# Modulation rows beside the branch mixture, six block-product pairs in the first feed-forward stage, ten in the second

## What is computed

```python
def hybrid_layer(x, c_act, ...):
    mod = c_act @ w_ada + b_ada                       # "modulation", 1 x 6144 per layer
    shift1, scale1, gate1, shift2, scale2, gate2 = jnp.split(mod, 6, axis=-1)
    h = modulate(rms_norm(x, norm1_g), shift1, scale1)
    ...
    y_br = jnp.einsum('bsnw,nwd->bsnd', branches, w_br)
    gates = jax.nn.sigmoid(h @ w_mg + b_mg).reshape(b, s, N_BRANCH, D_MODEL)
    mixed = jnp.sum(gates * y_br, axis=2) @ w_o       # the branch mixture
    x = x + gate1[:, None, :] * mixed
    h2 = modulate(rms_norm(x, norm2_g), shift2, scale2)
    u, g = jnp.split(h2 @ w_up, 2, axis=-1)           # 2 x 2816 columns
    u = causal_dwconv(u, w_conv, b_conv)              # three taps over the rows
    y = (jax.nn.silu(u) * g) @ w_down
    return x + gate2[:, None, :] * y
```

## Time and profile before

| what | us |
|---|---|
| median of 3 runs | 2886.88 |
| lowest and highest | 2886.42 and 7420.36 |
| the profiled execution, its time | 2883.55 |
| the profiled execution, its span | 2881.8 |

### The profile page before, as it was taken

How to read it: one execution, slowest core, us unless ns; L and a number is a source line. 1 busy time by engine, 2 the same in 40 slices (tenths; PEclk the granted TensorE clock), 3 DMA queues, 4 the chain that set the end, 5 groups by cost and what they waited for, 6 DMA issues and landing times.

```text
span 2881.8 us, 37607 instructions
## 1 busy us (share of the span) xinstructions
PE 2838.7 (99%) x15707; PEld 2402.4 (83%) x15707; DVE 1618.1 (56%) x2271; ACT 1183.9 (41%) x1809; POOL 1110.5 (39%) x458
## 2 busy tenths in 40 slices
PE   8999999999999999999999999999999999999999
PEld 5777888888888887788898989888999877789998
DVE  6444572467665624422266766647668466676683
ACT  4335333342333424532244435344334466443433
POOL 2332345334444332344434234443334423333432
PEclk9999999999999999999999999999999999999999
DMA  8331353346564422233233333333333322233332
GB/s 258 104 105 50 107 193 110 95 150 201 190 197 124 118 74 59 74 95 96 87 103 88 95 99 100 102 95 92 99 104 102 107 70 66 73 94 97 106 104 76
DMA packets 507293, 314.27 MB, mean 109 GB/s; under 512 B 14290, under 2 KB 478836, under 8 KB 506868
## 3 DMA queue, kind: packets, MB, share of 16 engines
q1 hardware_dynamic: 507124, 311.87, 36.7%
HBM read 309.73 MB, written 2.10 MB: 108 GB/s over the span
## 4 chain that ended last, share of the span: by engine, by line
PE 90%; DVE 6%; ACT 2%; DMA 1%; issue 1%; SPq 1%; POOL 0%; DVEq 0%; ACTq 0%
PE b L495 15%; PE b L497 15%; PE b L496 15%; PE o L495 4%; PE o L497 4%; PE o L496 4%; PE s L495 2%; PE s L496 2%; PE s L497 2%; PE b L1224 2%; PE b L1226 2%; PE b L1225 2%; PE s L1226 1%; PE s L1225 1%; PE s L1224 1%; PE b L1163 1%
## 5 line engine op out<-in xcount | busy, mean ns | idle before, releaser
L3370 POOL TENSOR_TENSOR lo<-raw,hi 128x1024 fp32r<-128x1024 f32 (+2 forms) x448 | 1108.2, 2483 | 1742.0 <-ACT hi L1501 1378.1
L1501 ACT ACTIVATE hi<-raw 128x1024 fp32r<-128x1024 f32 (+2 forms) x451 | 461.4, 1035 | 319.6 <-DMA raw<-in_w_up_dram 90.9
L495 PE MATMUL b<-HH,hi 128*128 128x512 f32 x1312 | 523.9, 399 | 0.0
L497 PE MATMUL b<-HH,lo 128*128 128x512 f32 x1312 | 511.4, 390 | 0.0
L496 PE MATMUL b<-HL,hi 128*128 128x512 f32 x1312 | 511.4, 390 | 0.0
L495 PEld LDWEIGHTS b<-HH,hi 128*128 128x128 f32 x1312 | 246.4, 188 | 58.4 <-issue 7.1
L497 PEld LDWEIGHTS b<-HH,lo 128*128 128x128 f32 x1312 | 246.3, 188 | 52.6
L496 PEld LDWEIGHTS b<-HL,hi 128*128 128x128 f32 x1312 | 246.6, 188 | 50.7 <-issue 1.4
L2521 DVE SCALAR_TENSOR_TENSOR AA<-raw,CA,AA 128x512 f32<-128x512 f32 x140 | 143.1, 1022 | 3.3
L495 PE MATMUL b<-FH,hi 128*128 128x512 f32 (+1 forms) x383 | 140.8, 368 | 0.0
L496 PE MATMUL b<-FL,hi 128*128 128x512 f32 (+1 forms) x383 | 140.6, 367 | 0.0
(11 more groups left out here) (645 smaller groups left out, 6891.8 us busy)
## 6 DMA issues: line engine op xcount, KB each, us to landing
raw<-in_w_up_dram SPq DMA_DIRECT2D x88, 512.0 KB, 4.0
raw<-in_w_ada_dram SPq DMA_DIRECT2D x80, 512.0 KB, 4.9
raw<-in_w_in_dram SPq DMA_DIRECT2D x76, 512.0 KB, 4.0
raw<-in_w_mg_dram SPq DMA_DIRECT2D x48, 512.0 KB, 3.7
raw<-in_ffn_w_gate_dram SPq DMA_DIRECT2D x44, 512.0 KB, 3.8
raw<-in_ffn_w_up_dram SPq DMA_DIRECT2D x44, 512.0 KB, 3.9
raw<-in_w_down_dram SPq DMA_DIRECT2D x32, 448.0 KB, 3.9
raw<-in_ffn_w_down_dram SPq DMA_DIRECT2D x32, 448.0 KB, 4.1
```

The lines of the kernel that those rows point to most:

```text
L495: e.matmul(out, wh, xh, start=start and k == 0, stop=False)
L497: mm = e.matmul(out, wl, xh, start=False, stop=stop and k == last)
L1501: e.activation(t["hi"][:, c % NSLOT, 0:w], K.raw[:, c % NSLOT, 0:w], ACT.Copy).then_inc(*m.hi.up(c))
L3370: e.tensor_tensor(t["lo"][:, s, 0:w], K.raw[:, s, 0:w], t["hi"][:, s, 0:w].bitcast(F32), ALU.subtract).then_inc(*m.lo.up(n))
```

## The change

Three things change. The modulation rows of the second layer are no longer left to the first feed-forward stage: one generator goes on from the first layer's rows to the second's, and the branch mixture of the first layer takes 60 of its steps in place of 28. The first feed-forward stage then makes f = 14, 15, 16, 17, 19 and 20 as pairs (none before) and takes no modulation step at its last block (marked `BUSY`); its input sums stand inside the down group behind f = 7. The second stage has ten pairs in place of thirteen, spaced otherwise. And in all four stages ScalarE's silu of the block before a pair stands behind the copy of "mid" and no longer ahead of it.

```diff
-PAIRS_OF = ((), (6, 7, 8, 9, 10, 12, 13, 14, 15, 16, 17, 19, 20),
+PAIRS_OF = ((14, 15, 16, 17, 19, 20),
+            (7, 8, 9, 11, 12, 14, 15, 16, 18, 19),
             (5, 6, 7, 8, 9, 10, 12, 13, 14, 15, 16, 17, 19, 20),
             (5, 6, 7, 8, 9, 10, 12, 13, 14, 15, 16, 17, 19, 20))
...
-        ada = (y for q in range(4, 12) for y in P.ada(0, q)) if l == 0 else iter(())
+        ada = (y for k, q0 in enumerate((4, 0)) for q in range(q0, 12) for y in P.ada(k, q)) if l == 0 else iter(())
...
-        drain(beside(chain(P.mixing(l, 0, (1,)), *[P.mixing(l, dp, (0, 2, 1)) for dp in (1, 2, 3)]), ada, 28))
+        drain(beside(chain(P.mixing(l, 0, (1,)), *[P.mixing(l, dp, (0, 2, 1)) for dp in (1, 2, 3)]), ada, 60))
...
-        fill = fill_next()
-        weave(P.ffn(l), fill, False)
+        weave(P.ffn(l), ada, False)
...
-                    yield from self.project(ap, c0, key, freed)
+                    for _ in self.project(ap, c0, key, freed):
+                        yield BUSY if f == KF - 1 else None
...
-    def pair_copies(self, i, f):
+    def pair_copies(self, i, f, late):
...
                      scale=-1.0).then_inc(*m.atake.up(("mid", i, f)))
+        if late is not None:
+            self.ffn_silu(i, late)
         q.wait_ge(m.dense.at("mid5", i, f))
...
                     yield from self.tile()
+                    if (i, f, d) == (0, 7, 3):
+                        self.halves_high(i)
...
                     self.down_update(i, DOWN[f][0], d, gate)
+                    if i == 0 and f == 7:
+                        if d == 0:
+                            self.halves_whole(i)
+                        if d == 2:
+                            self.halves_sums(i)
+                        if d in (4, 6):
+                            self.halves_low(i, (d - 4, d - 3))
```

More of the change, by code:

```diff
@@ L420, in schedule @@
         P.order = BIG4
-        drain(beside(chain(P.mixing(l, 0, (1,)), *[P.mixing(l, dp, (0, 2, 1)) for dp in (1, 2, 3)]), ada, 28))
+        drain(beside(chain(P.mixing(l, 0, (1,)), *[P.mixing(l, dp, (0, 2, 1)) for dp in (1, 2, 3)]), ada, 60))
         P.mods(l, 1)
         drain(P.out_proj("w_o", l, P.x_norm(2 * l + 1)))
-        def fill_next(l=l, ada=ada):
-            yield from ada
-            if l + 1 < DEPTH:
-                for q in range(12):
-                    yield from P.ada(l + 1, q)
-        fill = fill_next()
-        weave(P.ffn(l), fill, False)
+        weave(P.ffn(l), ada, False)
         if l + 1 < DEPTH:
             P.mods(l + 1, 0)
-        weave(P.out_proj("w_down", l, P.x_norm(2 * l + 2)), fill)
+        weave(P.out_proj("w_down", l, P.x_norm(2 * l + 2)), ada)
         P.order = BIG3
@@ L2046, in late_tile @@
                 self.pair_high(i, g, part)
-        if f is not None:
-            self.ffn_silu(i, f)
     def ffn(self, i):
@@ L2053, in take @@
             self.ffn_jobs(i, j)
-            if j == 3 and PAIRS_OF[i]:
+            if j == 3 and i:
                 self.halves_high(i)
@@ L2065, in ffn @@
                 for j in (2 * f, 2 * f + 1):
-                    yield from self.tile()
+                    for _ in self.tile():
+                        yield BUSY if f == KF - 1 else None
                     self.ffn_jobs(i, j)
@@ L2072, in ffn @@
                 yield BUSY
-                self.pair_copies(i, f)
+                self.pair_copies(i, f, late)
                 if late is not None:
@@ L3016, in take @@
             self.ffn_jobs(i, j)
-            if PAIRS_OF[i]:
+            if i:
                 if j == 2:
```

## The result

| what | before | after |
|---|---|---|
| median | 2886.42 us (the runs beside the changed kernel) | 2899.21 us (5 runs, 2897.27 to 2899.68) |
| ratio after to before | | 1.0048, 95% interval 1.0037 to 1.0059 |
| the profiled execution | 2883.55 us, span 2881.8 | 2899.21 us, span 2897.4 |

What follows compares the result with a forecast made beforehand. TensorE, busy 2838.7 of 2881.8 us, was taken as the bound. Terms: second stage -6.0, first-stage gains -8.2, its new waits +15.6, `w_o` +1.1, sum +2.5 us; on the median 2886.88 this gave 2889, range 2876 to 2902.

Steps and rivals of the forecast that it cites:

- Second stage, -6.0: Second feed-forward stage: +2.4 us for three pairs fewer, -10.6 for losses gone, +2.2 for two run starts; sum -6.0.
- the 3.7 us and the clock stretch go: Second stage's head and first pairs: with f = 7 first, VectorE finishes its sums early, removing the 3.7 us and slow-clock losses.
- The rival that named this stage: Second stage keeps its waits at run starts 11 and 18 and the head's lag: -6.0 becomes -1, 2894 us; chance 0.06.
- First stage, the input sums, 3.5: Down group behind f = 7: VectorE ends 12.7 us late, slack 8.1, TensorE waits 3.5 us, ends 0 and 12.7.
- Pair 14, 2.9: First stage, start of pair 14: chunks issued late for want of slots, TensorE waits 2.9 us, ends 0 and 5.
- Pair 15, 7.0: First stage, pair 15: late chunks at its start and a late copy of "mid", 7.0 us, ends 1.2 and 10.
- The clock, 1.0: First stage: lower granted clock behind waits of over 2 us adds 1.0 us in all, not 1.6 apiece.
- Pairs at 0.8: Both stages: each pair saves 0.8 us; six more in the first give -4.8, three fewer in the second +2.4.
- the tail at -3.4: First stage's end: modulation rows end earlier, the bank is free but for 0.2 us, the clock stretch goes: -3.4 us.
- Mixture 0, `w_o` +1.1: First layer's mixture: the added steps are hidden, no wait; at `w_o` a late low part costs 1.1 us, ends 0 and 2.
- Most waits don't appear: First stage: VectorE catches up and chunks come earlier, only about four run-start waits remain: about -8.5 us, 2878; chance 0.28.
- VectorE and GpSimd block each other: Down group behind f = 7: GpSimd casts hold up the sums, 31.6 us in place of 21.4: +13.8, 2901; chance 0.12.

Runs made afterwards that it cites:

- rows_only: The changed kernel without the first stage's six pairs and input sums; modulation rows, the second stage's ten pairs and silu's place stay: 2876.35 us, 0.9974 times before.
- banks_of_before: The changed kernel with only the PSUM bank counter moved, 6 behind the first stage and 3 behind the second: 2890.26 us, 1.0020 times before.
- quiet_13: banks_of_before with no modulation step beside f = 13, its two chunks coming four steps later: 2896.35 us, 1.0039 times before.
- silu_only: The kernel before with only silu of the block before a pair moved behind the copy of "mid": 2883.07 us, 0.9996 times before.
- rows_split: Against the changed kernel: second layer's rows 4 to 11 made in that layer, twelve pairs in both stages, least recently used bank: 2881.55 us, 0.9991 times before.
- sums_spread: banks_of_before with the twelve input-sum instructions one at a time, four low parts behind tiles of f = 8 and 9: 2884.09 us, 1.0000 times before.
- split_last: rows_split with more pairs, first-stage pairs from f = 8, input sums one at a time behind the modulation rows, last folds later: 2872.90 us, 0.9959 times before.
- changed_again: The changed kernel run once more, unaltered, to see whether the lower clock comes at the same places: 2899.89 us, a single execution.

## Why the forecast was near, and where it was wrong

In all, 2.5 us were summed and over 13 came. The forecast is near as a time because the change is small against the whole, not because the sum of the change was right. The measured 2899.21 lies inside the range only because the range's upper end was set by the rival in which GpSimd blocks VectorE, and that rival is not what happened: here the range was lucky.

- **Second stage, -6.0.** Right as a sum (rows_only: -6.1, banks_of_before: -5.1) and wrong in this kernel: +3.2. The step that failed is "the 3.7 us and the clock stretch go": they go, but I asked only when VectorE is done for the first pair, and not which bank each tile takes once the first stage has pairs. What came in its place is the wait of 6.3 us for a bank at f = 4 and 2.7 us of lower clock behind it. The rival that named this stage (its waits stay, 2894) had the right stage and the wrong mechanism.
- **First stage, the input sums, 3.5 by the lag read from the ring.** The right path: 4.0 us of waits in the trace, through the late weight DMA. With the clock they cost 5.8 (6.4 without the pairs). The sums took 18.8 us of VectorE, not 21.4.
- **Pair 14, 2.9.** A wait of 2.2 us from the late slot, shown by quiet_13 and by VectorE's idle time ahead of the sums, and 1.6 of lower clock in the profiled execution. The chunks were issued at 761.65 and VectorE's first sum began at 767.31, 5.7 behind; 5.5 had been forecast.
- **Pair 15, 7.0.** 6.8 by the matmul starts: 3.3 at its start (2.6 forecast), 0.8 at the copy where 4.4 had been forecast, and 2.7 of lower clock. The chain itself came as forecast. Tile 6 began at 814.96; the sums of pair 16 and the copy of "mid" were forecast 19 and 23.7 us behind (833.96 and 838.7), timelines of VectorE and ScalarE:

```profile
834.14 1.21 DVE L2953 TENSOR_TENSOR ER<-raw 128x1024 f32<-128x1024 f32 x1
```

```profile
837.82 0.58 ACT L2030 ACTIVATE MP<-s 128x512 f32<-128x512 f32 x1
```

The copy ended at 838.40. TensorE had used up most of that time at the pair's start and at the lower clock, so little was left to wait. No experiment takes this pair apart; it is read from the trace.

- **The clock, 1.0.** Mis-sized: some 6 us in the first stage, and 2.7 in the second where none was forecast. Of the 6, 2.7 lie ahead of pair 15's copy and stand in the place of a wait, as the prediction had it ("a slower TensorE also lets VectorE catch up"). The waits alone (gaps between matmul starts) were 11.0 us where 14.6 had been forecast, so the first stage's sum came out nearly right by two errors of opposite sign.
- **Pairs at 0.8 and the tail at -3.4.** Measured 4.9 for six and 3.97. Of the tail, 1.5 is again clock: in silu_only a wait of 2.15 us at that place was followed by clock 1.00, and `w_down` took 18.8 in place of 20.3. Two things could have taken the wait away, the end of the modulation rows, as forecast, and the bank counter, which gives the tile another bank in after. quiet_13 tells them apart: there the tile and the one that holds its bank are as before (`o` for both), the rows have ended, and the wait is 0.19 us, the 0.2 of the forecast.
- **Mixture 0, `w_o` +1.1.** Right: no wait in the mixture, 0.95 at `w_o` (0.9 to 1.5 in the other kernels).
- **The rivals.** *Most waits don't appear*: refuted. *VectorE and GpSimd block each other*: the mechanism is real (last section), its size was not: the sums took 18.8 us, not 31.6. Its number, 2901, was near by accident.

Of what is left, the +0.67 in the second layer and the +0.8 at the end have a share of the bank counter too: after has a wait of 0.78 us at 1274.94 and one of 1.61 at 2300.70 that neither before nor banks_of_before has. The +0.95 ahead of `w_o` I can't put down to the change: that part took 525.4 to 527.2 in the fourteen traces.

## What to carry to other kernels

A resource handed out by a running counter makes far-away code part of every edit: count what the edit takes from it. Giving out the least recently used one took the wait out of the stages here and put another into the attention mixer, so the banks are to be compared for the whole program either way. On a queue shared by two streams, what mattered here is the longest lump between two uses of a slot, not the mean load: the same twelve instructions cost 5.8 to 6.4 us as lumps of four and nothing when spread. Optional work that shares the ring belongs where nobody's chunks are late for it, and moving it must be followed to the place where it lands.

## What was not expected of the hardware

The lower granted clock (1.2 of 2.4 GHz) is not fixed by the program. Two executions of the same kernel had it behind different waits of about 2 us. One place shows it best: ahead of the attention's output projection all fourteen traces have the same wait for VectorE, 1.88 to 1.90 us; in nine the lower clock followed and the first three tiles took 18.04 to 18.09 us, in five (before, after, rows_split, sums_spread, split_last) it did not and they took 16.45 to 16.47. From the first stage on, every wait of 2.8 us or more in the fourteen traces had it beside or behind it. In three traces (rows_only, silu_only, changed_again) it also came in the attention mixer with no wait of over 0.4 us just ahead; in rows_only nine matmuls of 512 columns lost 1.7 us there:

```profile
2399.60:2403.00 3.40, 3.40 (x9) 2.62 (x9) 1.87 (x3) 2.93 (x8) 0.34 (x1) 0.50 0.04 11
```

From the first stage on it cost 1.5 to 3.0 us each time. Three such stretches more or fewer, an estimate from these prices, make a single profile differ by some 5 us, and of two profiles that differ by less, the gaps ahead of it are to be compared and not the spans. The Trainium skill ("TensorE: Matmul & The Clock Gate", Part 1) says that the number of slow matmuls at a kernel's start differs from run to run; the traces here show the same in the middle of one.

VectorE and GpSimd do block each other, once per cast. Timelines of POOL and VectorE in the trace of after:

```profile
685.93 2.40 POOL L3378 TENSOR_TENSOR lo<-raw,hi 128x896 fp32r<-128x896 f32 x1 [6.53 <-ACT hi L1496]
```

```profile
686.30 2.58 DVE L2521 SCALAR_TENSOR_TENSOR AA<-raw,CA,AA 128x512 f32<-128x512 f32 x1
```

The multiply-add takes 0.75 us alone. Here it began 0.4 us after a cast had begun and ended at 688.88, 0.55 behind the cast's end at 688.33: but for 0.2 us of its work it stood still until the cast was through. The Trainium skill ("SBUF — State Buffer", two separate sides) states an exclusive lock for the whole instruction, between a GpSimd instruction that reads SBUF and a VectorE one with two SBUF inputs, and the trace agrees but for these 0.2 us. What the rival got wrong is the count: a cast holds up the one instruction that it meets, not all that follow. Three of the twelve sums met one, 4.2 us above twelve times 1.22.
